# A rebuilt opening and a new chunk order in the input projection of a hybrid encoder layer

## The chip, the cores and the metric

The kernel runs on one core of a Trainium2 chip. The metric is device time of one execution, in microseconds (us); the lower the better. The engines are PE (TensorE, matrix products and transposes), DVE (VectorE), ACT (ScalarE), Pool (GpSimd) and SP (SyncE, which here issues most DMA transfers).

## What is computed

One encoder layer over a prompt of 256 rows and a sample of 2048 rows, all float32, width 1024; 18 tiles of 128 rows. One input projection feeds a Hyena mixer (a width-3 convolution, gating, and a long convolution through Fourier transforms) and a windowed attention; then an output projection and a feed-forward part. Cut to what matters here:

```python
def hyena_mixer(u, conv_w, conv_b, f_w1, f_b1, f_freq, f_w2, f_b2, f_w3, hy_skip):
    L = u.shape[1]
    uc = short_conv(u, conv_w, conv_b)
    x0, x1, v = jnp.split(uc, 3, axis=-1)
    h_f, h_b = implicit_filter(L, f_w1, f_b1, f_freq, f_w2, f_b2, f_w3)
    y = bidir_long_conv(x1 * v, h_f, h_b, hy_skip)
    return (x0.astype(jnp.float32) * y).astype(u.dtype)
...
def encoder_layer(x, norm1, w_in, ...):
    xn = rms_norm(x, norm1)
    proj = xn @ w_in
    hy_in = proj[..., :3 * HY_CH]
    ...
    y_hy = hyena_mixer(hy_in, ...)
    y_at = window_gqa(q, k, v, q_gain, k_gain, sink, rel_bias).astype(x.dtype)
    mixed = jnp.concatenate([rms_norm(y_hy, hy_gain), rms_norm(y_at, at_gain)], axis=-1)
    h = x + mixed @ w_out
```

## The kernel before

The change lies in `front`, the first of three phases, which fills the first 800 us or so; names there begin with `pr_` (projection), `fi_` (the filter and its transforms), `ur_` and `fs_` (transforms of u and of the filter), `sp_` (products of spectra and the way back) and `ir_` (the last transform, z).

**Precision.** Each float32 operand is split in a high part of a format that PE takes at full rate and the rest, the low part. A product is a triple of matmuls, high by high (L85), low by high (L86), high by low (L87).

**Rounds.** The projection is done in 6 rounds. A round holds six tiles of x, transposed, as `xhi` and `xlo`. Rounds 0 to 2 (hyena) have 8 units, rounds 3 to 5 have 10, over the same tiles again. A unit is 128 output columns: its weights come raw, ACT casts the high part (L1376), DVE makes the low one (L1659), into two places in turn. A unit has two chunks c = 0, 1 of 384 rows of x each; a chunk is 24 matmuls in a PSUM bank `pr_acc`, in a first and a second half of 12 (the first and last four of the eight blocks of 128 in the width). Each chunk is evicted by ACT (L1458) and DVE (L1718, L1720) with the three taps of the convolution; Pool multiplies for the gate (L914). PE transposes the gated product u (L1137) a few chunks later, and ACT copies it out (`ust`, L1431).

**Tiles.** Tile n of x is brought to place n % 5 of `xs` (L635). `norm` of a tile: squares and root on ACT (L1368, L1370), reciprocal and scale on DVE (L1653, L1655). `turn(r, j)`: PE transposes tile j of round r into two PSUM banks `pr_turned` (L1107), ACT copies it back over its place in `xs` (L1409), casts `xhi` from there (L1400), DVE subtracts to `xlo` (L1682). Turn 6 is one column of the next tile, the peek, without which the last column of the second chunk isn't known. The transposed tile is saved to `xkeep_dram` (L643), from where rounds 3 to 5 take it. x5 may be brought only when the save of place 0 is done and its low parts are made. PE does small idle matmuls (L1089) where it would wait in the opening.

**Order.** Each engine runs the same two generators with its own callbacks, and nothing at run time alters the order. `course()` is the main stream (norms, turns, weights, half chunks, evictions), `side()` the stream of the filter: two layers of waves (PE L1212, L1210, DVE L1748 to L1762, sines on ACT), steps of h (L1243, L1244, L1791, L1811) and of their transforms, then u steps, product and return steps, z steps. At each `yield` of the first, the other does one piece:

```python
    for _ in main:
        next(side, None)
    for _ in side:
        pass
```

```python
        def bring_x(n):
            if 5 <= n < NTT + 5:
                sp.wait_ge(x_saved, 16 * (n - 4))
            if n >= 5:
                sp.wait_ge(x_low, 2 * last_turn(n - 5) + (4 if (n - 5) // GT and (n - 5) % GT == 2 else 2))
```

## Time and profile before

| | |
|---|---|
| median of 3 runs | 2723.38 us (2722.14 to 2725.51) |
| profiled execution | 2724.04 us |
| its span | 2722.3 us |
| mean granted clock of PE | 0.984 |
| PE busy | 2619.3 us, 96% |
| DVE busy | 2106.0 us, 77% |
| ACT busy | 1372.8 us, 50% |
| Pool busy | 1230.2 us, 45% |

A time in the profile is counted from the start of the span. PE's busy time is made of matmuls that overlap each other, so 96% isn't PE at its peak; the granted clock is a share of full speed. An idle time before an instruction is put down to what released it. "Issue" is time in which an engine waited for nothing that the profile shows.

### The profile page before, as it was taken

The numbers are of one execution on the slowest core, as the hardware profiler recorded it, in microseconds if no ns is written. First come the engines' busy times: TensorE is split into PE (matmuls) and PEld (weight loads), VectorE is DVE, ScalarE is ACT, GpSimd is POOL, SyncE is SP. The second block draws the span as 40 slices with busy tenths as digits, with TensorE's granted clock in tenths as the row PEclk, the third lists the DMA queues.
The fourth block names the chain that finished last, engine by engine and source line by source line (L and its number), as shares of the span: only waits on it lengthen the run. The fifth ranks groups of instructions, "written<-read, shape, count | busy, mean of one in ns | idle before, by whom it ended". The sixth has DMA issues, their size and how long they took to land.

```text
span 2722.3 us, 39455 instructions
## 1 busy us (share of the span) xinstructions
PE 2619.3 (96%) x13881; PEld 2394.6 (88%) x13881; DVE 2106.0 (77%) x2518; ACT 1372.8 (50%) x2375; POOL 1230.2 (45%) x1182
## 2 busy tenths in 40 slices
PE   8999999999898999999999999899999989999998
PEld 6888989888797888878999999899999989999997
DVE  6765664678448777867888888988888888888887
ACT  5564544477448787764343434443434443443432
POOL 1655211112112454465687764455554444444443
PEclk9999999999998999999999999999999999999999
DMA  7688967899996454455444443543333355333332
GB/s 232 194 281 233 318 208 222 278 287 277 249 223 181 128 146 126 127 163 156 131 139 140 138 119 121 185 139 113 113 112 102 93 182 159 91 92 89 90 90 89
DMA packets 470044, 446.33 MB, mean 164 GB/s; under 512 B 54670, under 2 KB 377358, under 8 KB 469559
## 3 DMA queue, kind: packets, MB, share of 16 engines
q1 hardware_dynamic: 441960, 372.22, 47.4%
q0 software_dynamic: 27888, 71.58, 8.4%
q8 instruction: 112, 1.84, 0.3%
q14 instruction: 84, 0.69, 0.1%
HBM read 329.90 MB, written 113.79 MB: 163 GB/s over the span
## 4 chain that ended last, share of the span: by engine, by line
PE 84%; DVE 7%; DMA 4%; issue 2%; SPq 2%; ACT 1%; POOL 0%; DVEq 0%; ACTq 0%; POOLq 0%
PE ff_banks L85 17%; PE ff_banks L86 17%; PE ff_banks L87 17%; PE pr_acc L85 4%; PE pr_acc L86 4%; PE pr_acc L87 4%; PE am_mix L85 2%; PE am_mix L87 2%; PE am_mix L86 2%; PE pr_gen L85 2%; PE am_turn L2359 2%; PE pr_gen L87 1%; PE pr_gen L86 1%; DMA sp_k<-k_dram 1%; PE am_score L2346 1%
## 5 line engine op out<-in xcount | busy, mean ns | idle before, releaser
L3494 DVE TENSOR_TENSOR ff_h<-ff_h,ff_banks 128x1536 f32<-128x1536 f32 x231 | 402.9, 1744 | 6.2 <-PE ff_banks L87 5.4
L3330 ACT COPY ff_r<-ff_banks 128x384 f32<-128x384 f32 x198 | 94.9, 479 | 593.2 <-PE ff_banks L87 593.1
L3477 DVE TENSOR_TENSOR ff_dlo<-ff_dlo_raw,ff_dhi 128x512 fp32r<-128x512 f32 x231 | 212.8, 921 | 173.4 <-ACT ff_dhi L3360 173.1
L85 PE MATMUL ff_banks<-ff_xhi,ff_ghi 128*128 128x384 f32 x924 | 313.5, 339 | 13.8 <-DVE ff_silu L3454 8.1
L85 PE MATMUL pr_acc<-pr_xhi,pr_whi 128*128 128x386 f32 (+1 forms) x864 | 305.2, 353 | 12.7 <-DVE pr_xlo L1682 7.7
L87 PE MATMUL ff_banks<-ff_xhi,ff_glo 128*128 128x384 f32 x924 | 311.7, 337 | 0.0
L85 PE MATMUL ff_banks<-ff_xhi,ff_uhi 128*128 128x384 f32 x924 | 310.8, 336 | 0.7 <-ACT ff_r L3330 0.6
L86 PE MATMUL ff_banks<-ff_xlo,ff_ghi 128*128 128x384 f32 x924 | 311.2, 337 | 0.0
L86 PE MATMUL ff_banks<-ff_xlo,ff_uhi 128*128 128x384 f32 x924 | 310.6, 336 | 0.0
L87 PE MATMUL ff_banks<-ff_xhi,ff_ulo 128*128 128x384 f32 x924 | 310.0, 335 | 0.0
L3178 POOL TENSOR_TENSOR ff_act<-ff_act,ff_silu 128x384 f32<-128x384 f32 x99 | 116.6, 1177 | 419.6 <-issue 234.1
L86 PE MATMUL pr_acc<-pr_xlo,pr_whi 128*128 128x386 f32 (+1 forms) x864 | 298.0, 345 | 0.0
L87 PE MATMUL pr_acc<-pr_xhi,pr_wlo 128*128 128x386 f32 (+1 forms) x864 | 296.7, 343 | 0.0
L85 PE MATMUL ff_banks<-ff_dhi,ff_ahi 128*128 128x512 f32 x693 | 273.4, 395 | 9.7 <-issue 5.8
L86 PE MATMUL ff_banks<-ff_dlo,ff_ahi 128*128 128x512 f32 x693 | 273.5, 395 | 0.0
L87 PE MATMUL ff_banks<-ff_dhi,ff_alo 128*128 128x512 f32 x693 | 273.4, 394 | 0.0
L3481 DVE TENSOR_TENSOR ff_alo<-ff_act,ff_ahi 128x384 fp32r<-128x384 f32 x225 | 250.2, 1112 | 0.0
L85 PEld LDWEIGHTS ff_banks<-ff_xhi,ff_ghi 128*128 128x128 f32 x924 | 173.7, 188 | 22.1 <-DVE ff_silu L3454 9.1
L85 PEld LDWEIGHTS pr_acc<-pr_xhi,pr_whi 128*128 128x128 f32 x864 | 167.3, 194 | 22.4 <-DVE pr_xlo L1682 8.6
L86 PEld LDWEIGHTS ff_banks<-ff_xlo,ff_ghi 128*128 128x128 f32 x924 | 173.8, 188 | 5.9
L85 PEld LDWEIGHTS ff_banks<-ff_xhi,ff_uhi 128*128 128x128 f32 x924 | 173.3, 188 | 5.4 <-ACT ff_r L3330 0.9
L86 PEld LDWEIGHTS ff_banks<-ff_xlo,ff_uhi 128*128 128x128 f32 x924 | 173.5, 188 | 4.3
(353 smaller groups left out, 6692.2 us busy)
## 6 DMA issues: line engine op xcount, KB each, us to landing
ff_glo_raw<-w_gate_up SPq DMA_DIRECT2D x132, 256.0 KB, 3.0
ff_ulo_raw<-w_gate_up SPq DMA_DIRECT2D x132, 256.0 KB, 3.0
ff_dlo_raw<-dsum_dram SPq DMA_DIRECT2D x132, 256.0 KB, 2.7
pr_raw<-w_in SPq DMA_DIRECT2D x108, 256.0 KB, 5.8
ff_dlo_raw<-w_down SPq DMA_DIRECT2D x99, 256.0 KB, 2.6
sp_k<-k_dram SPq DMA_DIRECT2D x64, 256.0 KB, 5.6
pr_xs<-x SPq DMA_DIRECT2D x18, 512.0 KB, 5.7
xkeep_dram<-pr_xs SPq DMA_DIRECT2D x18, 512.0 KB, 4.5
```

Source lines behind the costliest of these rows:

```text
L85: pe.matmul(out, still[0], moving[0], start=start, stop=False, skip_group_check=goes_on)
L86: pe.matmul(out, still[0], moving[1], start=False, stop=False, skip_group_check=goes_on)
L87: return pe.matmul(out, still[1], moving[0], start=False, stop=stop, skip_group_check=goes_on)
L2346: pe.matmul(out, still, kk[:, c % 2, 0, h // 4, o], start=True, stop=False)
L2359: last = pe.transpose(turn[:, b, j * P:(j + 1) * P], prob[:, half_index(n, 4 * half) % 3, j, kb * P:(kb + 1) * P], ident[:])
L3178: pool.tensor_tensor(block, block, silu[c][:], ALU.mult).then_inc(tempered, 1)
L3330: act.copy(kept[n][:], bank(X)).then_inc(copied, 1)
L3477: dve.tensor_tensor(dlo[d_slot(n)][:], din[d_slot(n)][:], dhi[d_slot(n)][:].bitcast(F32), ALU.subtract).then_inc(d_low, 1)
L3481: dve.tensor_tensor(alo[n % AR][:], acts[:, STILL[k]], ahi[n % AR][:].bitcast(F32), ALU.subtract).then_inc(a_low, 1)
L3494: dve.tensor_tensor(to, to, lowered_all(k), ALU.add).then_inc(added, 1)
```

## The change

1. **A sixth place for x** (`sixth`, where a later table of the filter will lie). x5 goes there and waits for nothing; the first tile that waits for an old place is x6.
2. **Round 0's turns** leave out ACT's copy: `xhi` and `xlo` are both made from the PSUM banks, which PE may write again when the low parts are made. For the save, Pool adds `xhi` and `xlo` back into the place, 128x1024, six times. Pool's two loads of Fourier tables stand behind these.
3. **The first loads** come in another order (below). The filter's constants follow save 1, and w3 and the first decay rows come at turn 6.
4. **Chunk order.** Units 0 and 1 of every round run abreast: (0,0), (1,0), (0,1), (1,1), then the other units as before. Unit 1's weights are prepared at the round's first chunk, unit 2's at its fourth. Turn 3 stands behind the first half of the first chunk; turns 4 to 6 follow later than before. A norm's squares (ACT) and scale (DVE) may stand apart.
5. **The side stream** starts at the first yield instead of behind two chunks. It has further yields behind `weigh_step` 0 and 16 and in `first_z`; the high and low parts of octets 0 and 1 are made behind product step 1. The u rows of tiles 16 and 17 (the prompt) are fetched early, to a place of their own. The peek of rounds 0 to 2 is kept for 3 to 5.

The diff, cut to what is spoken of:

```diff
+    def abreast(r, i):
+
+        return i < 2
+
+    def place_of(r, i, c):
+        return i // 2 * 4 + 2 * c + i % 2 if abreast(r, i) else 2 * i + c
+
     def event(r, i, c):
-        return 2 * (first_unit(r) + i) + c
+        return 2 * first_unit(r) + place_of(r, i, c)
+
+    def chunks(r):
+        return sorted(((i, c) for i in range(units_of(r)) for c in range(2)), key=lambda ic: place_of(r, *ic))
+
+    def unit_end(n):
+
+        r = max(r for r in range(ROUNDS) if first_unit(r) <= n)
+        return event(r, n - first_unit(r), 1) + 1
...
         norm(3)
+        turn(0, 2)
         for r in range(ROUNDS):
-            end = units_of(r) - 1
+            order = chunks(r)
+            end, goes_on = len(order) - 1, r < ROUNDS - 1
             if r:
                 lift(r, 3)
                 seam(r)
-                evict(r - 1, units_of(r - 1) - 1, 1)
+                evict(r - 1, *chunks(r - 1)[-1])
+                yield
+                norm(GT * r + GT - 1)
                 yield
             else:
-                turn(0, 2)
-            turn(r, 3)
-            if r == 0:
+                turn(0, 3)
                 norm(GT - 2)
-            norm(GT * r + GT - 1)
-            if r:
+                norm(GT - 1)
+            for at, (i, c) in enumerate(order):
+                n = first_unit(r) + i
+                if n + 1 < UN and c == (abreast(r, i) and i % 2):
+                    weights(n + 1)
+                now[0] = event(r, i, c)
+                u_turn(now[0])
+                first_half(r, i, c)
+                if at == 0:
+                    turn(r, 3 if r else 4)
+                    if goes_on:
+                        norm(GT * r + GT)
+                if at == 1:
+                    turn(r, 5 if r else 6)
+                if c and 1 <= i <= 4 and goes_on:
+                    squares(GT * r + GT + i)
+                if at == end and goes_on:
+                    turn(r + 1, 1)
                 yield
-            for i in range(units_of(r)):
-                n = first_unit(r) + i
-                if n + 1 < UN:
-                    weights(n + 1)
-                now[0] = event(r, i, 0)
-                u_turn(now[0])
-                first_half(r, i, 0)
-                if i == 0:
-                    turn(r, 4)
-                    if r < ROUNDS - 1:
-                        norm(GT * r + GT)
-                yield
-                if i == 0:
-                    turn(r, 5)
-                second_half(r, i, 0)
-                evict(r, i, 0)
-                if i == 0 and peeks(r):
+                if at == end and goes_on:
+                    turn(r + 1, 2)
+                second_half(r, i, c)
+                if at == end and goes_on:
+                    break
+                if at == end:
+                    yield
+                if c and 1 <= i <= 4 and goes_on:
+                    scale(GT * r + GT + i)
+                evict(r, i, c)
+                if at == 0:
+                    turn(r, 4 if r else 5)
+                if at == 1 and r and peeks(r):
                     turn(r, 6)
-                if i == end and r < ROUNDS - 1:
+                if at == end - 1 and goes_on:
                     turn(r + 1, 0)
...
+    sixth = Place(nc, "fi", 184000).sb("sixth", [P, D])
...
-        if rd < NG and j == GT:
+        if rd == 0 or rd < NG and j == GT:
             return turned[:, h, :].rearrange("p (k c) -> p k c", k=4)
-        return xs[:, (GT * rd + j) % 5, 512 * h:512 * h + 512].rearrange("p (k c) -> p k c", k=4)
+        return spot(GT * rd + j)[:, 512 * h:512 * h + 512].rearrange("p (k c) -> p k c", k=4)
+
+    def spot(n):
+
+        return sixth[:] if n == GT - 1 else xs[:, n if n < 5 else (n - 1) % 5, :]
+
+    def x_arrival(n):
+
+        return (skip_in, 16) if n == GT - 1 else (x_in[n], 16) if n < 5 else (x_in[(n - 1) % 5], 16 * ((n - 6) // 5 + 2))
+
+    def before_in_spot(n):
+        return n - 6 if n < 11 else n - 5
...
-        while now[0] < 2:
-            yield
+             first_u, u_step, product_step, return_step, first_z, z_step, eighth_parts, z_parts, octet_parts, opening):
+
+        yield
         wave(0, 0)
...
+            if t in (0, N2):
+                yield
...
+            if j == 1:
+                for t in range(2):
+                    octet_parts(t)
+                    yield
...
+            if n > GT - 1:
+                was = before_in_spot(n)
+                if was < NTT:
+                    sp.wait_ge(x_saved, 16 * (was + 1))
+                sp.wait_ge(x_low, 2 * last_turn(was) + (4 if was // GT and was % GT == 2 else 2))
+            sem, count = x_arrival(n)
+            sp.dma_start(spot(n), x[n * P:(n + 1) * P, :] if n < NTT else xkeep_dram[n - NTT]).then_inc(sem, 16)
...
+        def later_constants():
             for d in range(2):
-                sp.dma_start(w3in[64 * d:64 * d + 64].rearrange("p a c -> p (a c)"), f_w3).then_inc(f_consts, 16)
+                sp.dma_start(w3in[64 * d:64 * d + 64].rearrange("p a c -> p (a c)"), f_w3).then_inc(g_in, 16)
             for s in range(2):
                 sp.dma_start(dec[:, s, :], decay[ORDER[s]]).then_inc(dec_in[s], 16)
 
         def turn(rd, j):
             if 1 <= j < GT:
                 save_x(rd, j - 1)
-            if rd == 0 and j == 1:
+            if rd == 0 and j == 2:
                 constants()
+            if rd == 0 and j == GT:
+                later_constants()
...
+            n = GT * rd + j + 5 + (rd == 0)
+            if n < ROUNDS * GT and (rd or j < GT - 1):
...
+            sp.wait_ge(weighted, NTT)
+            sp.dma_start(prompt_u[:], u_rows[LS:T].rearrange("(t p) c -> p t c", p=P)).then_inc(skip_in, 16)
...
         bring_x(0)
+        sp.dma_start(ident[:], ident_in).then_inc(ident_here, 16)
         sp.dma_start(gbc[:], norm1.partition_broadcast(P)).then_inc(gbc_in, 16)
         bring_x(1)
-        sp.dma_start(ident[:], ident_in).then_inc(ident_here, 16)
+        bring_x(2)
         bring_w(0)
-        for n in range(2, 5):
+        for n in range(3, GT):
             bring_x(n)
         bring_w(1)
...
+        def turn(rd, j):
+            if rd or j == GT:
+                return
+            o = slice(place(rd, j), place(rd, j) + P)
+            pool.wait_ge(x_low, 2 * j + 2)
+            pool.tensor_tensor(spot(j).rearrange("p (k c) -> p k c", k=KT), xhi[:, :, o].bitcast(F32), xlo[:, :, o].bitcast(F32), ALU.add).then_inc(x_copied, 2)
...
-                if j < GT:
+                if rd and j < GT:
...
-                act.wait_ge(unit_done, 2 * (n - 1))
+                act.wait_ge(unit_done, unit_end(n - 2))
...
-            if (rd >= NG or j < GT) and (rd == 0 or j != 3):
+            if rd and j < GT and j != 3:
+                if rd == 1 and j == 0:
+                    act.wait_ge(x_copied, 2 * GT)
                 lift(rd, j)
             for h in range(2):
                 if rd < NG:
-                    if j < GT:
+                    if rd and j < GT:
...
+            dve.wait_ge(returned, 2 * NJ)
```

How the order moves. First SP, which issues the transfers: in the kernel before, from the first save to the sixth tile of x (`xkeep_dram` is a save, L658 to L664 are the constants).

```order
L643 DMA xkeep_dram<-pr_xs 128x1024
L658 DMA pr_cw<-conv 128x48
L658 DMA pr_gq<-gains 128x2
L658 DMA pr_ones<-t_block_ones 128x128
L660 DMA fi_zt<-t_z 33x2304
L660 DMA fi_w_80<-f_w 33x64
L660 DMA fi_w_81<-f_w 64x64 x2
L660 DMA fi_cols<-f_cols 64x3 x2
L662 DMA fi_w3in<-f_w 64x1024 x2
L664 DMA fi_dec<-t_decay 128x512 x2
L643 DMA xkeep_dram<-pr_xs 128x1024
L635 DMA pr_xs<-x 128x1024
```

And with the change, from the fourth tile on:

```order
L689 DMA pr_xs<-x 128x1024 x2
L689 DMA fi_sixth<-x 128x1024
L706 DMA pr_raw<-w_in 128x4x128 x2
L697 DMA xkeep_dram<-pr_xs 128x1024 x2
L712 DMA pr_cw<-conv 128x48
L712 DMA pr_gq<-gains 128x2
L712 DMA pr_ones<-t_block_ones 128x128
L714 DMA fi_zt<-t_z 33x2304
L714 DMA fi_w_81<-f_w 33x64
L714 DMA fi_w_82<-f_w 64x64 x2
L714 DMA fi_cols<-f_cols 64x3 x2
L689 DMA pr_xs<-x 128x1024
```

The sixth tile (`fi_sixth`) stands ahead of all saves; two saves and nine constants stand ahead of the seventh (L689, `pr_xs`, behind `fi_cols`), where w3 and decay are no longer.

Second ACT, the opening, from the first turn to the first weights (`whi`), before:

```order
L1409 COPY pr_xs<-pr_turned 128x512 x2
L1400 CAST pr_xhi<-pr_xs 128x4x128 x2
L1368 ACTIVATE pr_junk,pr_stat<-pr_xs 128x1024
L1370 ACTIVATE pr_stat<-pr_stat,pr_eps 128x1
L1409 COPY pr_xs<-pr_turned 128x512 x2
L1400 CAST pr_xhi<-pr_xs 128x4x128 x2
L1376 CAST pr_whi<-pr_raw 128x1024
```

and with the change:

```order
L1477 CAST pr_xhi<-pr_turned 128x4x128 x2
L1439 ACTIVATE pr_junk,pr_stat<-pr_xs 128x1024
L1441 ACTIVATE pr_stat<-pr_stat,pr_eps 128x1
L1477 CAST pr_xhi<-pr_turned 128x4x128 x2
L1447 CAST pr_whi<-pr_raw 128x1024
L1439 ACTIVATE pr_junk,pr_stat<-pr_xs 128x1024
L1441 ACTIVATE pr_stat<-pr_stat,pr_eps 128x1
```

The copies are gone and the casts read `pr_turned`, the PSUM banks.

Third PE, before, from the end of the first half of chunk (0,0) to the start of its second half (L1107 the transposes of tiles 4 and 5, L1089 idle matmuls):

```order
L87 MATMUL pr_acc<-pr_xhi,pr_wlo 128x386
L1089 MATMUL pr_gen<-fi_out 128x384 x6
L1107 MATMUL pr_turned<-pr_ident,pr_xs 128x128 x8
L1089 MATMUL pr_gen<-fi_out 128x384 x6
L1107 MATMUL pr_turned<-pr_ident,pr_xs 128x128 x8
L85 MATMUL pr_acc<-pr_xhi,pr_whi 128x386
L86 MATMUL pr_acc<-pr_xlo,pr_whi 128x386
L87 MATMUL pr_acc<-pr_xhi,pr_wlo 128x386
```

and with the change, from the end of chunk (0,0) to the first half of (1,0):

```order
L87 MATMUL pr_acc<-pr_xhi,pr_wlo 128x386
L1160 MATMUL pr_gen<-fi_out 128x384 x6
L1178 MATMUL pr_turned<-pr_ident,fi_sixth 128x128 x8
L1283 MATMUL pr_gen<-fi_zt,fi_w_81 64x384 x3
L85 MATMUL pr_acc<-pr_xhi,pr_whi 128x386
L86 MATMUL pr_acc<-pr_xlo,pr_whi 128x386
L87 MATMUL pr_acc<-pr_xhi,pr_wlo 128x386
```

Tile 5's transposes and the filter's first wave (L1283) now stand between the whole chunk (0,0) and the first half of (1,0), and no longer ahead of the second half of (0,0).

## Rows read from the trace of the kernel before

**Rows 1.** The page: chain of waits by engine, and DMA issues (KB each, us to landing)
```profile
PE 84%; DVE 7%; DMA 4%; issue 2%; SPq 2%; ACT 1%; POOL 0%; DVEq 0%; ACTq 0%; POOLq 0%
...
xkeep_dram<-pr_xs SPq DMA_DIRECT2D x18, 512.0 KB, 4.5
```

**Rows 2.** PE's waits, 39 to 800 us: total us, times, longest
```profile
PE pr_gen L85 <- DVE sp_pb L1872: 9.2, 6, 3.8
PE pr_acc L85 <- DVE pr_xlo L1682: 7.7, 3, 4.2
PE pr_gen L85 <- DVE ir_zlo L1888: 5.5, 1, 5.5
PE pr_acc L85 <- issue: 5.0, 2, 2.5
PE pr_gen L85 <- DVE ur_ulo L1832: 4.3, 2, 3.7
PE pr_turned L1107 <- ACT pr_ust L1431: 2.8, 1, 2.8
...
PE pr_gen L1243 <- DVE fi_h L1811: 2.5, 1, 2.5
```

**Rows 3.** Windows of PE: length, busy us, granted clock, DMA share, GB/s
```profile
50.00:110.00 60.00, 52.52 (x254) 0.94 0.46 130
160.00:165.00 5.00, 4.56 (x17) 0.66 1.06 404
391.20:396.00 4.80, 4.76 (x14) 0.50 1.14 338
698.60:703.00 4.40, 4.33 (x12) 0.50 0.79 185
527.00:650.00 123.00, 114.23 (x600) 0.96 1.07 291
```

**Rows 4.** PE's timeline, opening: start us, us, line, operation, [idle before]
```profile
23.39 0.78 PE L85 MATMUL pr_acc<-pr_xhi,pr_whi 128*128 128x386 f32 x1
...
47.67 0.45 PE L85 MATMUL pr_acc<-pr_xhi,pr_whi 128*128 128x386 f32 x1
...
49.99 2.15 PE L1212 MATMUL pr_gen<-fi_zt,fi_w 33*64 33x384 f32 x6
```

**Rows 5.** The chain of waits, 0 to 60 us: start us, us, what
```profile
2.12 7.56 DMA pr_ident<-t_ident
...
15.49 0.60 SPq L660
...
19.68 8.93 DMA pr_xs<-x
```

**Rows 6.** ACT's timeline, opening
```profile
10.42 1.07 ACT L1409 COPY pr_xs<-pr_turned 128x512 f32<-128x512 f32 x2
11.38 1.16 ACT L1400 CAST pr_xhi<-pr_xs 128x512 fp32r<-128x512 f32 x2
...
28.63 1.06 ACT L1368 ACTIVATE pr_junk<-pr_xs 128x1024 bf16<-128x1024 f32 x1 [4.49 <-DMA pr_xs<-x]
```

**Rows 7.** DVE's timeline, opening and one row at 142 us
```profile
10.56 1.28 DVE L1655 SCALAR_TENSOR_TENSOR pr_xs<-pr_xs,pr_stat,pr_gbc 128x1024 f32<-128x1024 f32 x1
12.04 1.29 DVE L1682 TENSOR_TENSOR pr_xlo<-pr_xs,pr_xhi 128x512 fp32r<-128x512 f32 x2 [0.20 <-ACT pr_xhi L1400]
...
45.47 1.22 DVE L1659 TENSOR_TENSOR pr_wlo<-pr_raw,pr_whi 128x1024 fp32r<-128x1024 f32 x1
...
47.78 1.47 DVE L1748 TENSOR_SCALAR fi_arg<-pr_gen,fi_cols 64x1152 f32<-64x1152 f32 x1 [1.03 <-PE pr_gen L1212]
...
142.45 1.94 DVE L1682 TENSOR_TENSOR pr_xlo<-pr_xs,pr_xhi 128x512 fp32r<-128x512 f32 x2 [0.23 <-ACT pr_xhi L1400]
```

**Rows 8.** Groups of Pool by form: count, busy us, mean ns, idle before
```profile
L3134 POOL TENSOR_TENSOR ff_ulo_raw<-ff_ulo_raw 128x512 f32<-128x512 f32 x33 | 52.8, 1601 | 7.5 <-DMA ff_ulo_raw<-w_gate_up 5.0
...
L914 POOL TENSOR_TENSOR pr_cx<-pr_cx 128x384 f32<-128x384 f32 x20 | 31.2, 1562 | 100.6 <-DVE pr_cx L1720 100.5
```

More of the change, by code:

```diff
@@ L196, in edge_highs, with edge_lows @@
         return sum((k != NG) + 2 for k in range(1, r + 1))
-    def edge_lows(r, seam=True):
-        return sum((0, 1, 3, 2, 1, 3)[k] + 2 for k in range(1, r + 1)) - 2 * (not seam)
+    def edge_lows(r):
+        return sum((0, 1, 3, 2, 1, 3)[k] + 2 for k in range(1, r + 1)) - 2 * (not peeks(r))
     def turn_number(r, j):
@@ L334, in front @@
     eps = pr.sb("eps", [P, 1])
+    peeked = Place(nc, "pr", 227616).sb("peeked", [P, 2, NG - 1, KT], F32R)
     cx_at = pr.end
```

159 lines of the change are left out of this document (87 added, 72 removed).

## The prediction

> **What bounds the kernel now.** The chain of waits comes first: PE holds 84% of it and DMA 4% [rows 1], so a change pays only where PE idles or runs slowly. The list of PE's waits from 39 to 800 us, the front phase behind its opening, comes second [rows 2]; with its smaller lines it adds up to 48.3 us, and the reader should see by which line each wait was ended. A pause costs more than itself. The windows show PE's granted clock at 0.50, its 1.2 GHz level, just behind the long pauses [rows 3]; at that level half of the window is lost: 2.4 us of the 4.8 at 391, 2.2 of the 4.4 at 698; the window at 160 (0.66 of 5.0) loses 1.7. The opening is read third, from PE's timeline: first products at 23.39 [rows 4]. What held it afterwards is in the chain [rows 5] and in ACT's row at 28.63 with 4.49 of idle time before it [rows 6]: the sixth tile of x was issued at 19.68, behind a save and twelve constants, and took 8.93 to land.
>
> From 800 us on nothing is touched, so all gain has to come out of the first 800.
>
> **The opening.** Before, ACT passes over a tile three times: 1.06 for the squares, 1.07 for the copy (two instructions together), 1.16 for the casts [rows 6], and the small reads and roots between bring it to some 3.8 us; the first tiles come at that pace. The change takes the copies away: 2.7. DVE needs 1.28 for the scale and 1.29 for the low parts [rows 7], 2.7 with the reciprocal. So a tile comes about 1 us sooner, three to four times by the first product. The identity, which took 7.56 from its issue at 2.12 [rows 5] and held the first transposes, is now second in the queue and lands 1 to 2 us sooner. Casts from PSUM instead of SBUF I cost at the same 1.16, since the copy that read PSUM took 1.07 for as much; between 1.07 and twice that, the nearer row decides. First product: 23.39 − 3.5 = about 20 (bounds 18.5 and 23.4; the first weights now stand behind three tiles of x, not two).
>
> The sixth tile needs no old place and stands ahead of the saves, so its pause goes. What is late next is the seventh, x6, whose first column closes the second chunk of each unit. It waits for the first save, and that for the first Pool addition. No row shows an addition of 128x1024 on Pool. The nearest is the two-input addition of 128x512, 1.60, twice is 3.2; the upper end is the 384-column product, 1.56, scaled to 4.2 [rows 8]; the lower is DVE's pair, 1.29. I take 3.2. The first low parts are ready at about 11.7, the sum at 15, the save (4.5 to landing [rows 1]) lands near 20. Save 1 and nine constants at 0.60 each [rows 5] come next, so x6 is issued at about 25, lands at 30, is normed, transposed and peeked at 36. Meanwhile PE has three half chunks, tile 5 and a wave, then the second half of chunk (1,0) at 41 and the two last halves parked.
>
> Before, 72 products and one wave are done at 49.99; 12 products take 2.32 there and a wave the 2.1 between [rows 4]. After, the three first half chunks and one wave lie before 41; with 36 more products (6.5) and a gap of about 1 the same work, and a second wave besides, is done at 46.6, so at 44.5 without that wave. **Opening: −5.5** (bounds −9 and +2: the latter if the additions take 4.2 and x6 slips to 37).
>
> Here a rule is weighed. DVE's low parts take 1.29 a pair alone and 1.94 at 142.45, beside a Pool product [rows 7]; now six Pool additions lie beside DVE's work. I charge nothing, since DVE has idle time between tiles; 0.65 for two tiles is inside the bound. The Trainium skill, "GPSIMD Engine Reference", section 4.1 Engine selection, gives an elementwise addition of a tile to VectorE, since GpSimd is about twice as slow with two inputs; section 8, Key points, says that GpSimd shares its SBUF interfaces with VectorE, with contention where a DVE instruction has two SBUF inputs. The trace's 1.94 agrees. By the first the addition would be an estimated 2 × 1.22 = 2.4 us and x6 0.8 sooner; by the second the low parts, now with one input in PSUM, would keep 1.29 beside an addition and only the scales would suffer.
>
> **The filter's first waves.** The side stream starts at its first turn instead of after two chunks: DVE's wave work starts at about 37 instead of 47.78 [rows 7]. In the window 50 to 110 PE is idle for 60 − 52.5 = 7.5, nearly all of it for this chain, and the clock (0.94) costs 3.6 [rows 3]. Of the 10.9 us that the chain starts sooner 5.5 are the stream's own. Of the rest not all can count: ACT gets nine table loads instead of seven, and w3 arrives later. **−4** (0 and −11).
>
> **The turns at the start of a round.** Tile 3 is now turned behind the first half chunk, with the last norm ahead of it. Round 1: the wait for the u copy (2.8) with 1.7 of clock, **−4.5** [rows 2, 3]. Round 2: half of the line "issue" (2.5) and the same clock, **−4.2**. Round 3: 4.2 of xlo's 7.7 and 2.4 of clock, 6.6; but PE then has 48 products instead of 60 before the first u step, whose latency does not shrink, and the pause there grows by the 2.3 of 12 products and some clock: **−3.1**. The extra turn of the side stream at its tiles 0 and 16 removes a wait of 2.5 for h [rows 2]: **−2.5**.
>
> **The u, product and z chains.** DVE's waits for ulo (4.3), the other 3.5 of xlo and pb (9.2) [rows 2] are 17, with two losses of clock 21. Most are latency of round trips through DMA, whose share is 1.07 from 527 to 650 [rows 3]. Prompt rows fetched early, and octets 0 and 1 prepared behind product step 1, help only at the head: **−5** (0 and −12). At the start of round 5 the other half of "issue" (2.5) and z's 5.5 with 2.2 of clock hang together: from the last return to z runs a latency that PE bridges with 60 products instead of 36, so I count 24 × 0.19 = **−4.5**, not 11.
>
> **What is added.** Units 0 and 1 run abreast, so the place of unit 2's weights is free only one chunk (24 products, 4.6 us) before its use, at six round starts. In it lie ACT's eviction and cast and DVE's eviction and low weights; by the 512- and 1024-column rows of the same engines an estimated 0.58 + 1.06 + 1.3 + 1.22 = 4.2 [rows 6, 7], just hidden as long as nothing queues ahead on DVE. I charge 0.8 six times: **+5**. The peek row kept for rounds 3 to 5 and Pool's table loads behind its additions cost nothing under PE's chunks; without that cover they are two casts of a few columns, and one load's wait.
>
> **Sum:** −5.5 − 4 − 4.5 − 4.2 − 3.1 − 2.5 − 5 − 4.5 + 5 = −28.3. The profiled execution took 2724.04 (span 2722.3), 0.7 above the median of the three, so the forecast is 2695.7 by its time, and I say 2695 for the median.
>
> **Rivals.**
> (a) *The latencies swallow it.* The u, product and z chains are paced by DMA, and what is gained upstream is waited off there. For it: the share of 1.07, and pb as the largest line. Against: the opening and rounds 0 to 2 lie 100 us of full work before. The three terms from round 3 on go, 3.1 + 5 + 4.5 = 12.6, which leaves −15.7, or 2708; with an opening worth nothing 2713, up to 2722. Say 2714.
> (b) *Slower: the weights of unit 2 come late.* At each of the six starts DVE has low parts, evictions and the side stream's pair queued ahead of the low weights. Two more wide operations (1.22) there, one beside Pool (0.65 more), make some 3.5 of wait, and the clock behind it costs 2.4: 6 × 5.9 + 3 for PE's stretched side steps = 38 against 33 saved: 2729, up to 2736. It decides from 5.5 a start. Against: a side step of PE usually stands between the chunks and gives the queue 1 to 2 us more.
> (c) *More than counted.* The pauses of the u and product chains go too (another 7), z's 4, the filter's 4, and nothing new is added: −28.3 − 20 with the 5, about 2675 to 2665; say 2672.
> (d) *The rebuilt opening doesn't do what it says:* the additions take 4.2, saves slip, and PE waits for x6 as it did for the sixth tile. Opening +2 instead of −5.5: 2703.
>
> **How the numbers follow.** Forecast 0.50 (its own range 2684 to 2708), (a) 0.20, (b) 0.12, (c) 0.13, (d) 0.05. A measurement of this kernel can tell about 0.2%, 5.4 us, from no change. Below 2718: the forecast, (c), (d) and most of (a), 0.82; within 5.4 of 2723: the rest of (a) and the best of (b), 0.08; above 2729: 0.10, all of it (b). The range, 2674 to 2722, leaves out half of (c) below, and (b) and the last of (a) above.
>
> **What the changed profile would show.** First product at 19 to 21, no pause for the sixth tile, x6 normed at 30 to 32; 72 products and one wave by 45; no wait for the u copy at round 1, no "issue" wait at round 2; waits for unit 2's low weights under 1 us each. The forecast is wrong if PE waits for them over 3 us at several starts (b), if the waits for ulo, pb and zlo together stay above 17 (a), or if Pool's additions take over 4 us each (d).

## The result and the profile after

| | before | with the change |
|---|---|---|
| median | 2722.57 us (2716.81 to 2727.05, 20 runs) | 2729.85 us (2722.62 to 2733.72, 20 runs) |
| profiled execution, its span | 2724.04, 2722.3 us | 2725.23, 2723.4 us |
| ratio, 95% interval | | 1.0023, 1.0017 to 1.0030 |

The change makes the kernel slower by 0.23%, some 6 to 7 us. The forecast was 2695, with a range of 2674 to 2722: it is wrong in sign, and the result lies above the range.

The page's chain of waits has PE at 82%, 84% before [rows 1]:

```profile
PE 82%; DVE 8%; DMA 4%; SPq 2%; issue 2%; POOL 1%; ACT 1%; DVEq 0%; ACTq 0%; POOLq 0%
```

PE's waits from 39 to 800 us, the list that answers to [rows 2] (total, times, longest):

```profile
PE pr_acc L85 <- DVE pr_xlo L1767: 13.3, 2, 11.8
PE pr_gen L85 <- DVE ir_zlo L1983: 8.0, 1, 8.0
PE pr_gen L85 <- DVE sp_pb L1967: 7.5, 6, 3.2
PE pr_gen L85 <- DMA fi_table_b<-t_p_fwd: 5.2, 1, 5.2
PE pr_gen L1314 <- DVE fi_h L1883: 3.9, 2, 2.0
...
PE pr_turned L1178 <- ACT pr_ust L1508: 3.2, 1, 3.2
...
PE pr_turned L1208 <- issue: 1.8, 1, 1.8
```

Of the pauses that the change aimed at, "issue" fell from 5.0 to 0.7 ahead of products and the wait of 2.5 for h to 0.8, and the wait for ulo is gone. In their place stand a pause of 11.8 in one piece, one of 8.0 where there were 5.5, a new one of 5.2 for a table, and the u copy's 3.2 (2.8 before) at another round. Pauses over 0.3 us between 39 and 800 us add up to 57.8 us, 48.3 before. A wait of 2.1 for an eviction (`pr_cx`, at 78.0) is new as well.

Windows of PE (length, busy, granted clock, DMA share, GB/s) show that round 1 keeps most of its clock, 0.75 at 160 where [rows 3] has 0.66 (PE is busy all 5.0; the slow part follows a new wait of 2.0 for h at 157.9), and PE at the 1.2 GHz level behind the pause of 11.8:

```profile
50.00:110.00 60.00, 53.95 (x280) 1.00 0.61 177
160.00:165.00 5.00, 5.00 (x25) 0.75 0.96 340
533.30:537.50 4.20, 4.18 (x13) 0.50 0.49 126
```

Where the time went is read by marks. The 108 chunks of the projection come in both kernels with the same number of products ahead, so the start of chunk 4, 8, ... is a common mark. The table takes them from PE's timelines; the last column is the prediction's term.

| stretch of chunks | what lies there | before, us | after, us | difference | predicted |
|---|---|---|---|---|---|
| start to 4 | opening | 57.99 | 58.16 | +0.2 | −5.5 |
| 4 to 12 | filter's waves | 60.15 | 56.83 | −3.3 | −4 |
| 12 to 20 | start of round 1 | 77.19 | 76.24 | −1.0 | −4.5 |
| 20 to 28 | filter, prompt | 65.23 | 66.94 | +1.7 | −2.5 |
| 28 to 36 | start of round 2 | 55.38 | 59.15 | +3.8 | −4.2 |
| 36 to 52 | start of round 3 | 92.72 | 90.90 | −1.8 | −3.1 |
| 52 to 68 | u chain | 110.40 | 101.89 | −8.5 | −5 in all |
| 68 to 72 | start of round 4 | 34.29 | 42.13 | +7.8 | (in the −5) |
| 72 to 84 | products | 105.65 | 106.71 | +1.1 | (in the −5) |
| 84 to 92 | start of round 5, z | 61.63 | 62.91 | +1.3 | −4.5 |
| 92 to 107 | end of the front phase | 98.41 | 100.38 | +2.0 | 0 |
| sum | | | | +3.2 | −33.3, and +5 for weights |

So the change wins 15 us in four stretches, and gives back 18 in the others, most of it at the starts of rounds 2 and 4. In this pair of profiles the front phase is 3.2 us longer; the medians differ by 7.3. A second profile of the changed kernel (below) is 2.7 longer at the same mark. Most of the gap between 3 and 7 is that of single executions to their medians: the profiled one of the changed kernel is 4.6 below its median (2725.23 and 2729.85), that of the kernel before 1.5 above (2724.04 and 2722.57). Behind the mark single profiled executions differ by up to 7 us with the same code: 1900.5 from the start of chunk 107 in adds_twice, 1907.3 in adds_small (both below).

The marks have a spread of their own. Five profiles below (the change, again, peek_first, seq45, mix) have the same code up to chunk 48. They lie at 57.75 to 58.16 at chunk 4, but at 314.11 to 317.32 at chunk 36, and the stretch from 28 to 36 takes 56.4 to 59.2 in them. So a difference of 1 to 3 us in one stretch is not shown by one pair of profiles. The missing gain of the opening, the filter's waves, the u chain (101.89 in eleven profiles) and the start of round 4 (42.1 and 42.2 in the change and again) are clear of that.

**The opening.** DVE's timeline, with scales (L1741), low parts from PSUM (L1774) and low weights (L1745):

```profile
12.67 1.28 DVE L1741 SCALAR_TENSOR_TENSOR pr_xs<-pr_xs,pr_stat,pr_gbc 128x1024 f32<-128x1024 f32 x1
13.87 1.28 DVE L1774 TENSOR_TENSOR pr_xlo<-pr_turned,pr_xhi 128x512 fp32r<-128x512 f32 x2
15.07 2.21 DVE L1745 TENSOR_TENSOR pr_wlo<-pr_raw,pr_whi 128x1024 fp32r<-128x1024 f32 x1
...
17.39 3.19 DVE L1741 SCALAR_TENSOR_TENSOR pr_xs<-pr_xs,pr_stat,pr_gbc 128x1024 f32<-128x1024 f32 x1
...
25.50 2.74 DVE L1741 SCALAR_TENSOR_TENSOR pr_xs<-pr_xs,pr_stat,pr_gbc 128x1024 f32<-128x1024 f32 x1
...
32.51 3.07 DVE L1741 SCALAR_TENSOR_TENSOR pr_xs<-pr_xs,pr_stat,pr_gbc 128x1024 f32<-128x1024 f32 x1
```

GpSimd's additions beside them, two in one row of 6.78, then one at a time:

```profile
12.71 6.78 POOL L984 TENSOR_TENSOR pr_xs<-pr_xhi,pr_xlo 128x1024 f32<-128x1024 f32 x2 [12.29 <-DVE pr_xlo L1774]
21.92 2.37 POOL L984 TENSOR_TENSOR pr_xs<-pr_xhi,pr_xlo 128x1024 f32<-128x1024 f32 x1 [2.43 <-DVE pr_xlo L1774]
24.77 2.39 POOL L984 TENSOR_TENSOR pr_xs<-pr_xhi,pr_xlo 128x1024 f32<-128x1024 f32 x1 [0.47 <-DVE pr_xlo L1774]
32.11 2.38 POOL L984 TENSOR_TENSOR pr_xs<-pr_xhi,pr_xlo 128x1024 f32<-128x1024 f32 x1 [4.95 <-DVE pr_xlo L1774]
```

And PE, which waits for the third tile's low parts, then starts products 2.6 us later than before (23.39 in [rows 4]), not 3.5 sooner:

```profile
21.33 1.94 PE L1178 MATMUL pr_turned<-pr_ident,pr_xs 128*128 128x128 f32 x8 [4.49 <-DVE pr_xlo L1774]
...
25.97 0.47 PE L85 MATMUL pr_acc<-pr_xhi,pr_whi 128*128 128x386 f32 x1
```

A scale is 1.28 in [rows 7]; beside an addition it is 3.19 and 2.74, the low weights 2.21 instead of 1.22. Low parts, which read one operand from PSUM, keep 1.28 (13.87, inside the first row of GpSimd). The clock adds to it: PE stood idle for 4.49 us before 21.33, and its granted clock is 0.51, the 1.2 GHz level, from 21.3 to 26.0. So the transposes there take 1.94 and the ten idle matmuls behind them 3.21, where adds_small (below), with 1.6 us of idle time and a clock of 1.00, has 1.16 and 1.79.

**The start of round 4.** ACT's timeline. The row at 531.22 is the eviction of chunk (1,0) (L1536), and behind it stand the peek column's casts (L1474):

```profile
517.00 1.05 ACT L1683 CAST sp_yhi<-sp_yf 128x1024 fp32r<-128x1024 f32 x1 [6.55 <-POOL sp_yf L1093]
...
531.22 0.67 ACT L1536 ACTIVATE pr_cx<-pr_acc,pr_cw 128x384 f32<-128x384 f32 x1 [9.58 <-DMA x_dram<-pr_cx]
531.79 0.28 ACT L1474 CAST pr_xhi<-pr_peeked 128x4 fp32r<-128x4 f32 x2
```

It waited 9.58 us for a store of x0 rows (`x_dram<-pr_cx`) to land, that of chunk (9,0) of round 3, whose place in `pr_cx` it overwrites. DVE had finished that row at 503.9. SP's timeline shows why the store came so late (issue start, length): 12 loads of the first products, then a load of x with its own wait, and only then the store, 21.6 us behind its row and 3.8 behind the moment from which ACT waited (521.6). It landed 5.7 later:

```profile
511.86 7.68 SPq L882 DMA_DIRECT2D sp_a<-a_dram  x12
...
520.84 3.41 SPq L689 DMA_DIRECT2D pr_xs<-xkeep_dram  x1
...
525.46 0.58 SPq L754 DMA_DIRECT2D x_dram<-pr_cx  x1
```

Last, the start of round 2. ACT waits 5.20 us for tile 17 (its load took 10.2 to land), whose norm the change puts first; the u copy (L1508) and tile 3's casts (L1477), for which PE waits, come behind:

```profile
291.51 1.06 ACT L1439 ACTIVATE pr_junk<-pr_xs 128x1024 bf16<-128x1024 f32 x1 [5.20 <-DMA pr_xs<-x]
...
293.83 0.47 ACT L1508 COPY pr_ust<-pr_turned 128x384 f32<-128x384 f32 x1
294.20 1.14 ACT L1477 CAST pr_xhi<-pr_xs 128x508 fp32r<-128x508 f32 x2
```

### The profile page after: what moved, and what is told of

It is laid out like the page before. It is cut to its first block, busy times and chain, and to the rows that moved or that the text cites. A ratio compares the mean times of both kernels' runs of the same rounds, so it can differ in the third digit from the quotient of the medians.

```text
span 2723.4 us, 39456 instructions
## 1 busy us (share of the span) xinstructions
PE 2608.4 (96%) x13881; PEld 2380.6 (87%) x13881; DVE 2113.7 (78%) x2522; ACT 1367.8 (50%) x2369; POOL 1247.1 (46%) x1188
## 4 chain that ended last, share of the span: by engine, by line
PE 82%; DVE 8%; DMA 4%; SPq 2%; issue 2%; POOL 1%; ACT 1%; DVEq 0%; ACTq 0%; POOLq 0%
PE ff_banks L85 17%; PE ff_banks L86 17%; PE ff_banks L87 17%; PE pr_acc L85 4%; PE pr_acc L86 4%; PE pr_acc L87 4%; PE am_mix L85 2%; PE am_mix L86 2%; PE am_mix L87 2%; DMA sp_k<-k_dram 2%; PE am_turn L2455 2%; PE pr_gen L85 1%; PE pr_gen L86 1%; PE pr_gen L87 1%; PE am_acc L2469 1%
```

## The experiments

Two theories stood against each other. **Places**: the loss sits in a few places, each a queue whose head waits for something (a store, a load) or an engine held up by another, and what is mended there is kept to the end. **Latency**, my rival (a): the chains behind round 3 are paced by DMA and swallow any gain. All ratios are to the kernel before, in fast runs; there are 4 runs of all_yield, 5 of all, all_again and adds_twice, 9 to 20 of the others.

| run | ratio | 95% interval | median us | start of chunk 4, 36, 72, 107 in its profile |
|---|---|---|---|---|
| before | | | 2722.57 | 57.99, 315.94, 553.35, 819.04 |
| the change | 1.0023 | 1.0017 to 1.0030 | 2729.85 | 58.16, 317.32, 552.24, 822.24 |
| again | 1.0027 | 1.0016 to 1.0038 | 2729.68 | 57.75, 316.07, 551.04, 821.73 |
| peek_first | 0.9995 | 0.9983 to 1.0007 | 2722.12 | 57.76, 314.11, 541.15, 814.62 |
| adds_small | 1.0008 | 0.9997 to 1.0019 | 2724.81 | 52.78, 309.99, 544.95, 815.28 |
| seq45 | 0.9981 | 0.9970 to 0.9992 | 2714.80 | 57.88, 314.67, 545.15, 811.21 |
| late_norm | 1.0005 | 0.9997 to 1.0014 | 2724.69 | 58.47, 314.62, 549.53, 820.56 |
| act_copy | 1.0015 | 1.0006 to 1.0024 | 2726.18 | 55.25, 314.11, 548.98, 819.71 |
| mix | 0.9973 | 0.9962 to 0.9983 | 2716.01 | 58.06, 316.47, 541.62, 810.26 |
| all | 0.9948 | 0.9935 to 0.9961 | 2708.15 | 54.30, 306.97, 534.13, 801.97 |
| all_again | 0.9935 | 0.9918 to 0.9953 | 2705.71 | 55.42, 306.48, 531.91, 800.98 |
| all_yield | 0.9910 | 0.9893 to 0.9926 | 2699.37 | 54.28, 301.55, 525.39, 791.69 |
| late_side | 1.0018 | 1.0007 to 1.0029 | 2728.09 | 58.70, 318.16, 539.44, 818.66 |
| adds_twice | 1.0049 | 1.0032 to 1.0065 | 2737.40 | 67.98, 326.17, 561.50, 831.47 |

### again

No edit.

> The changed kernel itself once more, for a second profile. Store theory (the eviction of the second chunk of rounds 4 and 5 waits for a store of the round before, and the peek's parts stand behind it): PE's pause at about 533 us, 11.8 in the first profile, comes again at 8 to 13, and the ratio is 1.002 to 1.003. If that pause was a chance of one execution it is under 5 and another pause carries the loss. Latency theory (the chains behind round 3 are paced by DMA and swallow any gain): pauses may move about, the ratio is the same.

The pause came again to the hundredth, 11.81 at 532.10, as did the tables' (5.7) and z's (8.3). The loss is built in.

### peek_first

```diff
+                if at == 1 and r >= NG and peeks(r):
+                    turn(r, 6)
                 evict(r, i, c)
                 if at == 0:
                     turn(r, 4 if r else 5)
-                if at == 1 and r and peeks(r):
+                if at == 1 and 0 < r < NG and peeks(r):
                     turn(r, 6)
```

> In rounds 3 to 5 the peek column's parts are put ahead of the eviction of chunk (1,0), nothing else. Store theory: PE can run chunk (0,1) while the eviction waits, so the pause of 11.8 falls to about 7 or splits, ACT's wait for the store stays at 8 to 10, and the time falls by 4 to 6 us, to about 2725. Latency theory: the pause moves to a later wait, time within 1 us of the changed kernel.

Two adjacent steps swapped in one queue bring the ratio from 1.0027 to 0.9995. ACT still waits for the store, 9.54, but the peek's casts (L1476) are through before:

```profile
516.61 0.29 ACT L1476 CAST pr_xhi<-pr_peeked 128x4 fp32r<-128x4 f32 x2
526.43 0.67 ACT L1538 ACTIVATE pr_cx<-pr_acc,pr_cw 128x384 f32<-128x384 f32 x1 [9.54 <-DMA x_dram<-pr_cx]
```

and PE's pause is 5.3 instead of 11.8 (its waits):

```profile
PE pr_gen L85 <- DVE sp_pb L1969: 10.6, 7, 4.9
PE pr_gen L85 <- DVE ir_zlo L1985: 7.3, 1, 7.3
PE pr_acc L85 <- DVE pr_xlo L1769: 5.3, 1, 5.3
```

The front phase ends 7.1 us sooner than in "again" (814.62 against 821.73). The latency theory said within 1 us. But the marks give the swap less than 7.1. Of these, 3.7 are there at chunk 68, ahead of round 4 (505.16 against 508.88; seq45, without the swap, is at 505.79). The start of round 4 wins 6.2 (35.99 against 42.16), and the stretch from 72 to 84 gives 3.6 of them back (110.80 against 107.21), where pb's wait rose from 8.1 to 10.6. So the marks leave the latency theory about half of this gain; that the kernel did get faster rests on the ratios, whose intervals are apart.

### adds_small

```diff
-    pool.tensor_tensor(spot(j)....rearrange(...), xhi[:, :, o], xlo[:, :, o], ALU.add)
+    pool.tensor_tensor(spot(j)....rearrange(...)[:, :, 0:1], xhi[:, :, o.start:o.start + 1], xlo[:, :, o.start:o.start + 1], ALU.add)
```

> GpSimd's six additions write one column of each of the eight blocks (128x8) instead of 128x1024, so the rows staged for rounds 3 to 5 are left incomplete; everything else stands. Contention theory (the additions hold up the scales of DVE, 3.2 us against 1.28): the scales are back at 1.28, the first product comes at about 21 instead of 25.97, and the whole opening 4 to 5 us sooner; the end 3 to 5 sooner if nothing swallows it. Latency theory: the opening is sooner, the end is not.

DVE's scales are 1.28 again:

```profile
12.29 1.28 DVE L1741 SCALAR_TENSOR_TENSOR pr_xs<-pr_xs,pr_stat,pr_gbc 128x1024 f32<-128x1024 f32 x1
...
16.07 1.29 DVE L1741 SCALAR_TENSOR_TENSOR pr_xs<-pr_xs,pr_stat,pr_gbc 128x1024 f32<-128x1024 f32 x1
...
21.50 1.28 DVE L1741 SCALAR_TENSOR_TENSOR pr_xs<-pr_xs,pr_stat,pr_gbc 128x1024 f32<-128x1024 f32 x1
```

and the first product comes at 20.60 (the prediction had "about 20" by its terms):

```profile
20.60 0.47 PE L85 MATMUL pr_acc<-pr_xhi,pr_whi 128*128 128x386 f32 x1
```

Chunk 4 starts at 52.78, 5.2 before the kernel before; the prediction's term was −5.5. So the opening was reckoned rightly in all but one thing, the additions' hold on DVE (with the clock behind it), which costs the whole gain: from the first product to chunk 4 both kernels take 32.2. The end keeps it too: chunk 107 is 6.5 sooner than in "again", and chunk 68 6.2.

### seq45

```diff
     def abreast(r, i):
-        return i < 2
+        return i < 2 and r <= NG
...
+                if at == 0 and not abreast(r, 0):
+                    turn(r, 3)
+                    turn(r, 4)
...
+                if at == 0 and not abreast(r, 0):
+                    turn(r, 5)
                 second_half(r, i, c)
```

> Units 0 and 1 run abreast only in rounds 0 to 3; rounds 4 and 5 take chunks (0,0), (0,1), (1,0), (1,1) with the turns where the kernel before has them. Store theory: no wait of ACT for the store of x0 rows at those starts, PE's pause at 533 under 4 us, z's wait near the 5.5 of before, and the time 10 to 14 us lower, about 2717. Latency theory: about 2728. If the weights of unit 2 had been the trouble at rounds 4 and 5, a wait for wlo would have gone too; there was none in the profile.

The time is where the store theory put it, 2714.8, but not by the way it said at round 4. ACT has no wait for a store there or at round 5 (its waits, 690 to 712 us):

```profile
ACT pr_cx L1543 <- PE pr_acc L87: 5.5, 2, 4.7
```

z's wait is down to 1.2. But PE still pauses at round 4's start, 9.5 us, now for the low parts of the peek (L1774), which stand on DVE behind those of tile 5 and an eviction (waits of PE):

```profile
PE pr_acc L85 <- DVE pr_xlo L1774: 11.0, 2, 9.5
PE pr_gen L85 <- DVE sp_pb L1974: 9.6, 7, 2.5
```

In sequence, PE has one chunk to do ahead of them, not two. ACT's casts of tile 5 stood 5.5 us behind `sp_yhi`, which waits for GpSimd's sum of the first product, and the two subtractions of its low parts, with both operands in SBUF, took 3.42 instead of 1.29 beside the next sum. That is a second blocked queue at the same place; in the changed kernel, too, ACT stands 6.55 us for this sum (517.00 above). For round 5 the sequence is better (chunk 84 to 92: 56.4 against 62.3 in peek_first). For round 4 abreast with the peek in front is 3.4 better up to chunk 72 (35.99 against 39.36), of which 2.6 are given back by chunk 84.

### late_norm

```diff
-                norm(GT * r + GT - 1)
...
                 if at == 0:
                     turn(r, 3 if r else 4)
+                    if r:
+                        norm(GT * r + GT - 1)
```

> The norm of a round's last tile goes back behind the turn of tile 3, as before the change; nothing else. Blocked-queue theory (at the start of round 2 ACT stands 5.2 us for tile 17, whose load took 10.2 us, with the u copy and tile 3's casts behind it): the waits for ust (3.2) and issue (1.8) at 294 to 298 go or fall under 2 together, the offset against the kernel before stays at about -4 at chunk 36 instead of +1.4, and the time falls by 4 to 6 us. Latency theory: the offset is better at chunk 36 and is lost again by round 4; the end within 1.5 us of the changed kernel.

ACT's timeline shows the u copy (L1509) at 287.07 and tile 3's casts at 287.44, 7 us sooner, and the wait for tile 17 behind them:

```profile
287.07 0.48 ACT L1509 COPY pr_ust<-pr_turned 128x384 f32<-128x384 f32 x1
287.44 1.15 ACT L1478 CAST pr_xhi<-pr_xs 128x508 fp32r<-128x508 f32 x2
291.45 1.06 ACT L1440 ACTIVATE pr_junk<-pr_xs 128x1024 bf16<-128x1024 f32 x1 [2.86 <-DMA pr_xs<-x]
```

The wait for ust is gone, but 3.2 of idle time ahead of a u transpose (L1209, "issue") stands in its place. Chunk 36 is at 314.62, 1.3 ahead of the kernel before and not the 4 expected, and inside the 314.11 to 317.32 of the profiles that don't have this edit. More runs together show a small gain: from chunk 32 to 36 late_norm, all and all_again, which have it, take 25.9 to 28.6, and the eight profiles with the norm where the change puts it (late_side, whose side stream lies otherwise, left out) 28.5 to 31.2. The ratio fell by 0.0022 against "again", some 6 us, as expected, the end mark by only 1.7 against the change; but the profiled execution here is 4.6 above its median, that of the change 4.6 below. A half miss: the time is as expected, the marks don't show where most of it is won.

### act_copy

```diff
-            pool.tensor_tensor(spot(j)..., xhi[:, :, o]..., xlo[:, :, o]..., ALU.add).then_inc(x_copied, 2)
...
-            if rd and j < GT and j != 3:
-                if rd == 1 and j == 0:
-                    act.wait_ge(x_copied, 2 * GT)
+            if j < GT and (rd == 0 or j != 3):
                 lift(rd, j)
```

> Round 0 turns as before the change: ACT copies PSUM back to the row place and casts from there, no GpSimd additions; sixth place, load order, chunk order all stay. Contention theory: DVE's scales are 1.28 again, but ACT's pace of 3.8 a tile is back; first product between the 20.6 without additions and 25.97, about 22.5, and the time 2 to 4 us below the changed kernel. If the copy on ACT was the dear part, as my prediction had it, the first product comes later than 25.97 and the time rises.

First product at 23.07, 2.9 sooner than with the additions, chunk 4 at 55.25. At these marks the old way, with ACT's copy, beats the new one; in time the two can't be told apart (1.0015, whose interval overlaps that of the change). The new load order and sixth place with the old turns are worth 2.7 (57.99 to 55.25); removing the copy is worth another 2.5 only if the rows are staged at no cost to DVE (52.78).

### adds_twice

Each addition stands twice, one behind the other.

> Each of the six GpSimd additions is done twice. Contention theory: twice the time in which DVE's scales are slow; first product 3 to 5 us later than 25.97, about 29 to 31, and the end 3 to 6 later. If the additions cost nothing (as I charged them), the first product stays at 26 and only x6 comes later, by 3.

First product at 28.04 (2.1 later, not the 3 to 5 I expected), but chunk 4 at 67.98, 9.8 later: the longer queue on GpSimd also holds the saves, and with them x6. The time rises by 0.22% against "again", some 6 us, and the end mark by 9.7, more than the 3 to 6 expected. Contention and lateness both grow with the additions; this run doesn't part them, adds_small and act_copy do for the first product.

### mix

peek_first's swap for rounds 3 and 4, seq45's order for round 5 alone.

> Abreast in rounds 0 to 4, in sequence in round 5, and the peek ahead of the eviction in rounds 3 to 5. Store theory: it has the shorter pause of peek_first at round 4 (about 5) and seq45's start of round 5 (no store wait, z near 5 or less); the two gains add, 7.6 + 3 to 5: about 2718. If both acted on one and the same pause: 2715 to 2722 with no gain over seq45.

The pauses are as expected (5.3 at round 4, no store wait at round 5) and chunk 107 is at 810.26, 4.4 sooner than peek_first. Against seq45 the gain is 1 us at the mark and nothing that the medians show (2716.0 and 2714.8, intervals overlap). At the mark, then, less than the sum: pb's waits rose to 12.5. That much the latency theory has right: mix wins 6.4 at the start of round 4 against "again" (35.74) and gives 4.6 back by chunk 84.

### all, and all_again

mix, late_norm and act_copy in one.

> mix, late_norm and act_copy together. If the three causes (store wait, blocked queue at round 2, contention in the opening) are separate places that nothing behind swallows, the gains add: about 11 + 5 + 3 below the changed kernel, 2710 to 2713, below both kernels. If the chains behind round 3 swallow what comes before them, it is no faster than mix.

> The combined version once more, beside all_yield on one chip: ratio 0.993 to 0.996 as in its first run (only 5 runs counted there), if the gain is its own and no chance of those runs.

0.9948 and 0.9935: the version is 0.5% and 0.65% faster than the kernel before, at 2708 and 2706, a little below the 2710 to 2713 expected. Against mix the front ends 8.3 us sooner, more than the 2.5 of act_copy and 1.7 of late_norm one by one (chunk 36 is 9.5 sooner). The gains of the opening and of round 2 are kept, as the places theory says.

### late_side

```diff
-        yield
+        while now[0] < 2:
+            yield
         wave(0, 0)
```

> The side stream starts behind two chunks again, as before the change; nothing else. My prediction put 4 us on the sooner start by 110 us. If that holds, chunk 12 comes 3 to 4 us later than in the changed kernel (118 to 119) and the end with it. If the start only shifts which step of the side stream meets which turn: chunk 12 within 1.5 us, and the pause at 533 changes, since other product steps then lie beside the start of round 4.

A miss of my prediction's reason. Chunk 12 comes at 116.25, only 1.3 later, so most of the gain at 50 to 110 us is not from the sooner start. What remains is the new chunk order and the other loads, which no run tries by themselves. The later start costs elsewhere (chunk 20 is 10.4 later, with these waits of PE) and wins it back at round 4, where the product steps no longer fall beside the turns and the pause of 11.8 is gone:

```profile
PE pr_gen L85 <- DVE sp_pb L1968: 13.3, 8, 4.3
PE pr_gen L1315 <- DVE fi_h L1884: 6.7, 3, 2.9
PE pr_gen L85 <- DVE fi_hlo_b L1873: 4.3, 1, 4.3
```

This run also tells what made the wait of round 4. Its order is abreast, with the same single chunk between store and eviction, yet ACT doesn't wait for the store: SP issues it at 519.16, now ahead of the 12 loads, and it has landed at 523.57, before chunk (1,0) is done (ACT and SP):

```profile
519.16 0.45 SPq L755 DMA_DIRECT2D x_dram<-pr_cx  x1
...
521.90 7.55 SPq L883 DMA_DIRECT2D sp_a<-a_dram  x12
...
527.01 0.68 ACT L1537 ACTIVATE pr_cx<-pr_acc,pr_cw 128x384 f32<-128x384 f32 x1 [4.25 <-PE pr_acc L87]
```

So the shorter distance alone doesn't make the wait. What differs is the place of the product loads in SP's queue; the later side steps have moved as well. At chunk 107 the run is 3.6 ahead of the changed kernel, in the medians within the intervals of it. Which side step meets which turn is worth more here than when the stream starts.

### all_yield

```diff
             if t in (0, N2):
                 yield
+        yield
         for k in range(2):
             prompt(k)
```

> The combined version with one more yield ahead of the two prompt steps of the filter, so that PE has one more half chunk before it wants the last piece of the prompt's table. If the 5.5 us wait for that load is a matter of the distance between issue and use, it falls to about 3 (12 products are 2.3 us) and the time by 1 to 3 us; if the load only lands when the 16 loads behind it let it, the wait stays 5 and the time too.

PE's waits: the table's fell from 5.5 to 3.2, as expected, and round 4's pause is 4.3:

```profile
PE pr_gen L85 <- DVE sp_pb L1975: 11.1, 9, 3.7
PE pr_acc L85 <- DVE pr_xlo L1775: 4.7, 2, 4.3
PE pr_gen L85 <- DMA fi_table_b<-t_p_fwd: 3.2, 1, 3.2
```

That the 16 filter loads behind the table held it up is ruled out: here SP issues the first of them at 241.30, when the last piece of the table has landed (240.59), and that piece still took 6.9. The time fell by more than expected, to 2699.37 (0.9910), the best of all kernels here, 0.9% under the kernel before. Chunk 36 is 4.9 sooner than in all_again, and chunk 107 by 9.3; the rest of that gain is again a different meeting of side steps and turns, which I had not worked out.

## Why the prediction was wrong, step by step

The terms together were to bring −28.3; at the start of chunk 107 the change stands at +3.2. The largest misses are round 2 (8.0 off), z (5.8), the opening (5.7) and the u and product chains (5.4). None of the three signs of being wrong that the prediction named came: no wait for low weights of unit 2 (b), the waits for ulo, pb and zlo together 15.5, under 17 (a), the additions 2.4 alone and 3.4 beside DVE, under 4 (d). What went wrong wasn't on its list.

- **The opening, −5.5.** The step that failed is "I charge nothing" for the additions beside DVE, with 0.65 for two tiles as the bound, from one row of 1.94 against 1.29. The rows of the changed kernel show scales of 3.19, 2.74 and 3.07 and low weights of 2.21 for 1.28 and 1.22. All else held: 20.60 for a predicted 20, 5.2 us for 5.5 with the additions cut down. Rival (d), with 0.05, had an opening without gain, but by additions of 4.2 and a late x6; PE did not wait for x6 (32.2 from the first product to chunk 4, as in adds_small). The error was to take the price from the instruction shown (low parts, which the change makes safe by reading PSUM) and not to ask for the ones left with two operands in SBUF, the scales.
- **The rule weighed there.** The Trainium skill, "GPSIMD Engine Reference", section 4.1 Engine selection, says that GpSimd is about twice as slow with two inputs, by which I estimated 2.4 us for an addition, against the 3.2 I took from the rows. Alone it takes 2.37 to 2.39, so the rule was the better price, and beside DVE 3.4 (6.78 for two). Section 8, Key points, has the contention for DVE instructions with two SBUF inputs: the traces agree (3.19 for 1.28, and 1.28 kept with one input in PSUM). I named this sentence and gave it no price. A price was to be had: the Trainium skill, "SBUF — State Buffer", Who interferes with whom, says that the two engines share one pair of ports, under an exclusive lock, that a DVE instruction with two SBUF inputs contends there with a GpSimd one that reads SBUF, and (of the DVE modes that use both its ports) that whoever issues first has the pair for the whole instruction and the other fully blocks. By that each scale or subtraction caught behind an addition loses up to an estimated 2.4 us and not 0.3, and the traces agree: the three scales lost 1.9, 1.5 and 1.8, the subtraction 1.0 (last section).
- **The filter's waves, −4.** 3.3 came, but late_side shows that the sooner start brings at most 1.3 of it. Right in size, mostly wrong in cause.
- **Round starts, −4.5, −4.2, −3.1.** Round 1: the wait for ust went, but a wait of 2.0 for h came just behind it, at 157.9, and kept most of the clock loss (0.75 at 160); −1.0. Round 2: I counted what the move of the turn takes away and not what the norm, moved with it ahead of the queue, waits for: 5.2 us for tile 17. The stretch is 3.8 longer here and 1.1 to 3.8 in the five profiles with this code; late_norm puts the norm back and gains 0.2% in time. The wait of 2.8 for ust did not vanish, it moved from round 1 to round 2. Round 3: −1.8 of −3.1.
- **The h wait, −2.5.** It fell to 0.8, but another wait for h rose, and all of them together are 5.6, 5.4 before. And a table of the prompt came too late, a term I didn't have. Before, its four pieces were issued from 248.02 on, took 3.0 to 3.4 to land, and were used at 253.34 without a wait. Now they were issued from 237.55 on, PE wanted them at 241.4, and they took 6.1 to 6.8; the last landed at 246.5. A piece of work more ahead of the use (all_yield) took 2.3 off the wait. The 16 filter loads behind them are not the reason (see all_yield); the transfers issued around them (weights, `tw_blocks`, the filter's stores) took 5.0 to 8.0 as well. What slowed them all stays open.
- **The u and product chains, −5.** The u chain gave 8.5, more than I allowed. Then the start of round 4 took 7.8, so from chunk 52 to 72 only 0.7 is won (144.0 against 144.7). The missing term is the eviction of the second chunk: abreast, (1,0) comes one chunk behind the store of the row place it overwrites, where it was two. Before, that store landed at 536.8 and ACT came to the eviction at 543.8. Now ACT was there at 521.6, and the store, behind the 12 product loads in SP's queue, was issued at 525.5 and landed at 531.1. Neither by itself makes the wait: the kernel before has the loads ahead of the store but the longer distance, late_side the shorter distance but the loads behind the store. seq45, with the old order, has no such wait either. The store ahead of the loads in the abreast order was not tried by itself. I had read the abreast order for the weights alone.
- **The weights, +5.** No wait for low weights of unit 2 is in the list; the term is 0. Rival (b), to which I gave 0.12 and 2729, has the right time by a mechanism that didn't happen. What did happen is its neighbour: the same abreast order, another buffer.
- **z, −4.5.** +1.3. The same store wait (8.29 on ACT at 707) stands ahead of z's casts in ACT's queue; PE's wait for z is 8.0, and 1.2 in seq45, where the store wait is gone (5.5 before).
- **Rival (a)**, latency, 0.20: refuted as the main cause by adds_small, whose gain reaches the end whole, and by all; in part true: of what peek_first and mix win at the start of round 4 the products behind it give back more than half (3.6 of 6.2, 4.6 of 6.4).

## What to carry to other kernels

When steps are reordered, list for every buffer that they write how many steps now lie between its last reader (a store to memory too) and its next writer, and compare that with the time from the row's completion to the landing of the transfer, the issuing queue included; here the landing was 5.7, but the store was issued 21.6 us behind its row, with 12 other loads ahead of it. In an in-order queue, a step that may wait long goes behind those that others wait for: one swap was worth 0.3%. Before giving GpSimd work that another engine does, look at what DVE does at that moment with two SBUF operands: here each such instruction, once caught behind an addition, stood until its end, and the addition behind it likewise.

## What the runs showed of the hardware

DVE instructions of 128x1024 with two operands in SBUF took 3.19 instead of 1.28 us (scale) and 2.21 instead of 1.22 (subtraction) beside GpSimd's two-input addition, and the addition 3.4 instead of 2.38. The scale that began at 12.67, 0.04 us before the addition, kept its 1.28. Low parts with one operand in PSUM kept 1.28. In adds_twice, where a scale began at 12.69, 0.02 us behind an addition, it took 3.43. In adds_small the additions of 128x8 take 0.22 alone; one that began at 12.34, 0.05 behind a scale, took 1.32 and ended 0.09 behind that scale, which kept its 1.28. The rows fit an exclusive hold by whichever began first, and not a shared rate. An addition ran from 32.11 to 34.49 and another to 19.49; the scales that began inside them, at 32.51 and 17.39, ended at 35.58 and 20.58, each 1.09 behind the addition's end, whatever their start (0.2 less than a scale takes alone), and the one at 25.50 at 28.24, 1.08 behind the end at 27.16. The other way round, the pair of 6.78 is two additions of 2.38 and some 2.0 of waiting: behind the scale that ended at 13.95, then behind the subtraction that ended at 17.28. ACT's casts from PSUM took no longer than from SBUF (1.05 to 1.16 a pair).
